# Sixteen expert weight slots refilled pair by pair, and 512-wide gate/up matmuls in a feed-forward

## The reference

```
def hier_moe(t, ...):            # 32 experts, hidden 512
    for e in range(N_EXPERTS):
        he = jax.nn.silu(t @ w_gate[e]) * (t @ w_up[e])
        y = y + combine[:, e:e + 1] * (he @ w_down[e])

def swiglu(x, w_in, w_out):      # 1024 -> 2 * 2816 -> 1024
    gate, up = jnp.split(x @ w_in, 2, axis=-1)
    return (jax.nn.silu(gate) * up) @ w_out
    # used as x = x + 0.5 * swiglu(rmsnorm(x, ...), ...), four times
```

## Time and profile before

| | |
|---|---|
| median of 3 runs | 1894.71 us (1894.43 to 1897.06) |
| profiled execution, its own time | 1897.47 us |
| its span, first to last instruction | 1895.6 us |
| TensorE (PE) busy | 1807.6 us (95%) |
| DVE busy | 938.3 us (49%) |
| ACT busy | 732.7 us (39%) |
| DMA | 441.92 MB, mean 233 GB/s |
| granted TensorE clock, mean | 0.983 |

### The profile page before, as it was taken

How to read it: one execution, slowest core, us unless ns; L and a number is a source line. 1 busy time by engine, 2 the same in 40 slices (tenths; PEclk the granted TensorE clock), 3 DMA queues, 4 the chain that set the end, 5 groups by cost and what they waited for, 6 DMA issues and landing times.

```text
span 1895.6 us, 29657 instructions
## 1 busy us (share of the span) xinstructions
PE 1807.6 (95%) x11498; PEld 1425.7 (75%) x11498; DVE 938.3 (49%) x1313; ACT 732.7 (39%) x1164; POOL 108.0 (6%) x121
## 2 busy tenths in 40 slices
PE   5999899999999879999999999999999998899998
PEld 2976544444434369998899998899989998779998
DVE  5773222222212265556877775545555554755554
ACT  2353212212212144444555554444444443754443
POOL 2010000000000000001212211000000001210000
PEclk8999899999999989999999999999999999999999
DMA  9966789999999966666554553556656665036663
GB/s 384 353 222 250 289 326 420 422 422 422 422 422 422 421 195 176 194 181 168 156 152 115 142 156 101 157 177 198 177 160 195 180 181 212 1 90 184 193 183 104
DMA packets 317570, 441.92 MB, mean 233 GB/s; under 512 B 12074, under 2 KB 270634, under 8 KB 289602
## 3 DMA queue, kind: packets, MB, share of 16 engines
q1 hardware_dynamic: 314418, 431.57, 66.0%
q0 software_dynamic: 2816, 8.45, 1.3%
q10 hardware_dynamic: 272, 1.05, 0.2%
HBM read 439.97 MB, written 1.05 MB: 233 GB/s over the span
## 4 chain that ended last, share of the span: by engine, by line
PE 79%; DMA 12%; DVE 4%; issue 2%; ACT 1%; POOL 1%; SPq 0%; POOLq 0%; DVEq 0%; ACTq 0%
PE PS L281 25%; PE PS L291 12%; PE PS L382 10%; DMA RAW<-w_up 9%; PE PS L2125 7%; PE PS L1712 4%; PE PS L2186 3%; PE PS L2099 2%; PE PS L158 2%; PE PS L1846 1%; PE PS L454 1%; DMA R<-w_down 1%; PE PS L528 1%; PE PS L511 1%; PE PS L719 1%
## 5 line engine op out<-in xcount | busy, mean ns | idle before, releaser
L281 PE MATMUL PS<-XH,LO 128*128 128x256 f32 x1344 | 380.3, 283 | 0.0
L281 PE MATMUL PS<-XL,HI 128*128 128x256 f32 x1344 | 380.3, 283 | 0.0
L281 PE MATMUL PS<-XH,HI 128*128 128x256 f32 x1344 | 379.9, 283 | 0.0
L203 DVE TENSOR_TENSOR LO<-RAW,HI 128x2048 fp32r<-128x2048 f32 x88 | 201.7, 2292 | 138.7 <-ACT HI L199 138.7
L281 PEld LDWEIGHTS PS<-XL,HI 128*128 128x128 f32 x1344 | 257.7, 192 | 3.1
L281 PEld LDWEIGHTS PS<-XH,HI 128*128 128x128 f32 x1344 | 257.7, 192 | 3.1
L281 PEld LDWEIGHTS PS<-XH,LO 128*128 128x128 f32 x1344 | 257.7, 192 | 0.0
L212 ACT ACTIVATE HI<-RAW 128x1024 fp32r<-128x1024 f32 x88 | 93.0, 1064 | 285.2 <-PE PS L291 285.2
L239 DVE TENSOR_TENSOR LO<-RAW,HI 128x1024 fp32r<-128x1024 f32 x88 | 107.5, 1225 | 186.5 <-ACT HI L212 186.5
L199 ACT ACTIVATE HI<-RAW 128x2048 fp32r<-128x2048 f32 x88 | 167.6, 1904 | 4.2 <-PE PS L1174 1.5
L291 PE MATMUL PS<-HI,HH 128*128 128x512 f32 x352 | 138.3, 393 | 0.4 <-DVE HL L247 0.2
(11 more groups left out here) (392 smaller groups left out, 3240.0 us busy)
## 6 DMA issues: line engine op xcount, KB each, us to landing
RAW<-ffn_w_in SPq DMA_DIRECT2D x176, 512.0 KB, 5.0
R<-w_gate SPq DMA_DIRECT2D x56, 1024.0 KB, 19.8
RAW<-ffn_w_out SPq DMA_DIRECT2D x88, 512.0 KB, 3.6
RAW<-a_w_in SPq DMA_DIRECT2D x69, 512.0 KB, 5.2
SPLIT<-w_up SPq DMA_DIRECT2D x31, 1024.0 KB, 21.9
RAW<-w_up SPq DMA_DIRECT2D x30, 1024.0 KB, 23.1
SPLIT<-w_down SPq DMA_DIRECT2D x30, 1024.0 KB, 17.9
R<-w_ada SPq DMA_DIRECT2D x24, 1024.0 KB, 10.7
```

The source lines that it names most:

```text
L203: v.tensor_tensor(M.LO[:, j, 0:2048], M.RAW[:, j, 0:2048], M.HI[:, j, 0:2048].bitcast(f32), ALU.subtract).then_inc(s.gu_lo[j], 1)
L281: m = e.matmul(GU[j][:, T * q:T * q + T], gu(w, j)[:, q, k, :], x[:, k, :], start=(k == 0 and n == 0), stop=(k == KT - 1 and n == 2))
```

## The change

**Experts.** The ring has sixteen slots in eight pairs: the six pairs of before, `MORE[0]` with `MORE[1]`, and `MORE[2]` with `MORE[3]`. They are refilled in the order `TURN`; pair p of loads waits for pair p - 8 to be used (`freed_by`), once for both loads. Since the place now differs from step to step, the 16 steps of SP's and of TensorE's program are written out where they were a loop. XH and XL are one tensor XHL, and their early users XH_SLOT and SPARE one XH_SPARE. The loads of norm_final and of the first feed-forward wait for 4, 0 and 2 loads of the last step.

```
+    TURN = (0, 1, 3, 4, 5, 6, 7, 2)
+    def freed_by(p):
+        return p - FIRST_PAIRS if p < FIRST_PAIRS + 2 else p - len(TURN)
...
+            for p in range(FIRST_PAIRS, PAIRS_IN):
+                sp.wait_ge(s.used, 2 * freed_by(p) + 2)
+                for x in range(2):
+                    first_load(2 * p + x)
...
-            with e.Fori(first // 2 or 1, end // 2 - 1) as i:
-                two_steps(i)
+                for i in range(end // 2 - 1):
+                    two_steps(i)
...
-            sp.wait_ge(M.steps.used, LOADS * (PAIR_STEPS - 1) + (8, 12)[j])
+            sp.wait_ge(M.steps.used, LOADS * (PAIR_STEPS - 1) + (0, 2)[j])
```

```
-                    for n, (w, x) in enumerate([(M.HI, XH), (M.HI, XL), (M.LO, XH)]):
-                        m = e.matmul(GU[j][:, T * q:T * q + T], gu(w, j)[:, q, k, :], x[:, k, :],
+                    e.matmul(GU[j][:, q].rearrange("p (w t) -> p w t", w=2), gu(M.HI, j)[:, q, k, :], XHL[:, k],
+                             start=k == 0, stop=False)
+                    m = e.matmul(HALF(j, 0)[:, q], gu(M.LO, j)[:, q, k, :], XH[:, k, :], start=False, stop=k == KT - 1)
...
+        def second_half(j, i):
+            a.activation(M.SECOND[:, j], HALF(j, 1), ACT.Copy).then_inc(s.silu[j], 1)
+        def step(j, i, following, after):          # ScalarE
+            second_half(j, i)
+            if following:
+                gu_high(*following)
+            silu(j, i)
+            if after:
+                dn_high(*after)
+            h_high(j, i)
...
+        def added(j, i):
+            v.tensor_tensor(M.GATE_UP[:, j], HALF(j, 0), M.SECOND[:, j], ALU.add).then_inc(s.h_done[j], 1)
+        def step(j, i, following, after):          # VectorE
+            added(j, i)
+            hidden(j, i)
+            if following:
+                gu_low(*following)
+            h_low(j, i)
+            if after:
+                dn_low(*after)
...
+        step(1, i - 1, (1, i), (0, i))             # ScalarE, i = 10
+        second_half(0, i)
         M.after(n_norm).first_high()
-        silu(1, FF_TWICE - 1)
+        silu(0, i)
+        dn_high(1, i)
+        h_high(0, i)
+        step(1, i, None, None)
```

More of the change, by code:

```diff
@@ L204, in gu_low, with dn_high @@
                         ALU.subtract).then_inc(s.gu_lo[j], 1)
-    def act():
[L207 to L212, removed]
-        def silu(j, i):
[L215 to L218, removed]
-            a.activation(M.HH[:, j], M.H[:, j], ACT.Copy).then_inc(s.hh_done[j], 1)
-        for j in range(2):
-            high_parts(j, 0, first=True)
+    def dn_high(j, i):
+        a.wait_ge(s.dn_in[j], i * 16 + (16 * u0 + 16))
+        a.wait_ge(s.dn_used[j], i + (u0 + 1))
+        a.activation(dn(M.HI, j), dn(M.RAW, j), ACT.Copy).then_inc(s.dn_hi[j], 1)
@@ L223, in act @@
         if f == 0:
             a.wait_ge(M.x_ready, 4)
[L225 to L230, removed]
+        first_silu()
+        gu_high(0, 1)
+        h_high(0, 0)
+        dn_high(1, 0)
+        with a.Fori(1, FF_TWICE - 1) as i:
+            step(1, i - 1, (1, i), (0, i))
+            step(0, i, (0, i + 1), (1, i))
+        i = FF_TWICE - 1
+        step(1, i - 1, (1, i), (0, i))
@@ L231, in act @@
+        second_half(0, i)
         M.after(n_norm).first_high()
-        silu(1, FF_TWICE - 1)
+        silu(0, i)
+        dn_high(1, i)
+        h_high(0, i)
+        step(1, i, None, None)
     def dve():
[L235 to L240, removed]
+        def added(j, i):
+            v.wait_ge(s.silu[j], i * 2 + (2 * u0 + 1))
+            v.tensor_tensor(M.GATE_UP[:, j], HALF(j, 0), M.SECOND[:, j], ALU.add).then_inc(s.h_done[j], 1)
@@ L251, in dve @@
             v.tensor_scalar(X[:, t], M.XNF[:, t], M.RSB[:, t:t + 1], None, ALU.mult).then_inc(M.x_ready, 2)
-        for j in range(2):
-            low_parts(j, 0, first=True)
+        dn_low(0, 0)
         hidden(0, 0, first=True)
[L255 to L259, removed]
+        h_low(0, 0)
+        gu_low(0, 1)
+        dn_low(1, 0)
+        with v.Fori(1, FF_TWICE - 1) as i:
+            step(1, i - 1, (1, i), (0, i))
+            step(0, i, (0, i + 1), (1, i))
+        i = FF_TWICE - 1
+        step(1, i - 1, (1, i), (0, i))
+        added(0, i)
+        hidden(0, i)
         M.after(n_norm).first_low()
-        hidden(1, FF_TWICE - 1)
+        h_low(0, i)
+        dn_low(1, i)
+        step(1, i, None, None)
         for n in range(4):
@@ L1917, in passes, with load @@
         extra = 1 if first else 0
-        def load(g, m, to=None, loaded=None):
+        def load(g, m, to, loaded):
             src = (gate, up, down)[m // 4][bass.ds(g * 2 + m % 2, 1), m // 2 % 2]
[L1921 to L1933, removed]
+            sp.dma_start(to, src.rearrange("e p n -> p (e n)")).then_inc(loaded, 16)
@@ L1935, in sync @@
         def sync():
             if first == 0:
[L1937 to L1960, removed]
+                first_pass_loads()
+                sp.wait_ge(s.used, LOADS * (PAIR_STEPS - 1) + 4)
+                sp.dma_start(M.NFR, A["norm_final"]).then_inc(M.mix.cx_in, 16)
+                return
@@ L2103, in w_loaded @@
         def w_loaded(i, odd, m):
[L2105 to L2111, removed]
+            if first == 0:
+                n = LOADS * (2 * i + odd) + m
+                at, loaded, count = home(n // 2, n % 2)
+                e.wait_ge(loaded, count)
+                return at
+            e.wait_ge(s.w_in[m // 2], i * (2 * 32) + 32 * (odd + 1 - PAIR_STEPS + pairs_on(m // 2)))
+            return SLOTS[m]
         def gate_up(i, odd):
@@ L2208, in pe @@
             if first == 0:
-                two_steps(0)
-            with e.Fori(first // 2 or 1, end // 2 - 1) as i:
-                two_steps(i)
+                for i in range(end // 2 - 1):
+                    two_steps(i)
+            else:
+                with e.Fori(first // 2, end // 2 - 1) as i:
+                    two_steps(i)
             it = end - 1
```

98 lines of the change are left out of this document (76 added, 22 removed).

## The result

The changed kernel takes 1886.01 us in the median of 5 runs (1883.86 to 1888.06). The kernel before took 1894.71 us in 5 runs beside it (1894.43 to 1899.48). The ratio is 0.9947 with a 95% interval of 0.9932 to 0.9961: 0.53% faster, some 10 us (the medians lie 8.7 apart), about half of the 20.2 that were forecast. The profiled executions took 1886.12 and 1897.47 us, 11.35 apart; what follows divides these.

A forecast was written before the change was run, and what follows sets the result against it. Experts were taken as bound by TensorE, then by DMA, the feed-forward by TensorE. Terms -8.35 - 14.0 + 2.1 = -20.2 us took 1894.71 to 1874.5 us; the 8-in-10 range was 1867 to 1889.

The forecast's parts named there:

- Thus none of the 8.35 us is left: Experts: sixteen slots let transfers start earlier, removing DMA's idle time between 245 and 275 us; -8.35 us.
- Edits at nothing: Experts: fetching TensorE's written-out steps as instructions costs nothing unless a fetch outlasts the work TensorE has queued; 0 us.
- A pair saves 2 x 119.8 - 229.2 = 10.4 ns: Feed-forward matmuls: one 512-wide replaces two 256-wide in each of 1344 pairs; -14.0 us in all.
- 1.9 us of cover are left: Feed-forward loop: other matmuls cover 8.3 us, so ACT's added copy and DVE's addition cost nothing in 80 steps.
- the chain of 6.4 us: Feed-forward step: ACT and DVE work between gate_up and its down product, summed with hops to 6.4 us.
- In the first step ... nothing: Feed-forward's first step: gu_high precedes h's high part, but the 3.5 us chain fits under gate_up's 5.6; costs nothing.
- The last down products: End of each feed-forward: copy and addition delay the last down product by 0.53 us, four times; +2.1 us.
- D: Rival, feed-forward loop: steps become bound by the chain through ACT and DVE; slower, 1916.5 us; chance 0.06.
- A: Rival, feed-forward: merged matmuls save nothing, as the long one's fixed part doubles with operand and target in two pieces; 1888.5 us; 0.12.
- C: Rival, feed-forward: the remaining 256-wide matmuls fall from 119.8 to 106.7 ns, 17.6 us more saved; 1856.9 us; chance 0.09.
- B: Rival, experts: earlier transfers bring nothing, as 14 loads ahead aren't possible or slots free too late; 1882.8 us; chance 0.09.
- the release by a w_down: Sign, end of experts: the last down product starts near 659.6 instead of 667.98, still waiting for a w_down load.

The follow-up runs named there:

- `e5_grouped`: Changed kernel with TensorE's expert steps 3 to 14 looped, plus each q's eight 512-wide matmuls before its eight 256-wide ones: 1876.96 us, ratio 0.9886.
- `e6_contiguous_x`: Changed kernel with TensorE's expert steps 3 to 14 looped, plus x's high and low halves side by side for each k: 1882.75 us, ratio 0.9922.
- the looped kernel: The changed kernel with TensorE's expert steps 3 to 14 in a loop of four steps, three turns, sixteen slots kept: 1882.06 us, ratio 0.9924.
- `e1_experts_only`: The changed kernel with the feed-forward of before, so only the experts' half of the change: 1891.46 us, ratio 0.9968 against the kernel before.

## Why the prediction was wrong

The direction and both mechanisms were right, and 1886.01 lies in the range, near its upper end. The size was off by a factor of two, and three steps of the working failed.

**"Thus none of the 8.35 us is left"** held: DMA ran full from 245 us, and the landings moved by 8.3 to 8.4 us. **"Edits at nothing: TensorE's steps written out must be fetched as instructions"** failed. The term was put at nothing, and the changed kernel loses 2.9 us of landings (3.06 - 0.12) with 10 fetches more. I asked only whether TensorE would wait for a fetch, and it doesn't. The fetch is itself a DMA transfer, and DMA had just been called the limit, at a share of 1.01. With nothing but the steps written out (12 fetches more) the kernel before lands its last load 1.8 us later (1.93 - 0.12); in the loop the last down product starts at 659.56, where the forecast had 659.4. That "the first steps of before were written out and ran at the same 28.20 us" was no evidence: there TensorE was the limit, not DMA.

**"A pair saves 2 x 119.8 - 229.2 = 10.4 ns"** was mis-sized: 6.8 measured. The rows were of matmuls among their own kind, x12 and x48; of alternating ones there was no row. With the rows' own conditions restored the pair saves 359.5 - 347.6 = 11.9 ns. The Trainium skill's rule of a fixed 2.5 ns ("TensorE: Matmul & The Clock Gate", section "Wait — 56ns, not 53.3ns?") agrees with neither: by it a pair would save 2.5, an estimate. Each matmul here has its own weights, and the fixed part was 10 ns and more (116.9 - 106.7).

**"1.9 us of cover are left, so the copy and the addition cost nothing in 80 steps"** failed in three of them, the ones that end in the second down product of the first, third and last feed-forward: 1.9 us. The cover itself was about right: a wait of ACT for the weights of 1.8 us opened no gap, waits of 2.12, 2.75 and 3.23 us opened 0.23, 0.58 and 1.06 us. But the chain of 6.4 us was summed from durations alone, and gu_high stands in it and waits for a load that had not landed. "In the first step ... nothing" held: the first down product had no gap.

**The last down products** were right, +0.53 forecast and +0.54 measured on average, by rows of each operation. That it agrees so closely is partly luck: one by one they were +0.61, +0.37, +0.43 and +0.74, since the forecast worked out the first feed-forward and took it four times. D's mechanism, the chain through ACT and DVE above its cover, showed itself in those three steps of 84 and not in the loop as a whole; A and C (0 or 23.5 ns per pair, against 6.8) fell. Of B the place was right: SyncE does get stuck in its issues, and no more than 12 loads were under way. But DMA stayed full with that, so it cost nothing. "DMA at 1.01 from about 241 us" and the gap at each last down product were seen; the release by a w_down, the step of 8.33 us and the 229 ns were not, and each of the three pointed at the failed step. Two of the signs of being wrong came too: a wait of TensorE for VectorE inside the loop, and a 256-wide matmul whose successor starts after 116.9 ns, not 120.

## What to carry over

Where DMA is the limit, count everything that goes through it, instruction fetches too: TensorE's steps written out added 10 to 12 here, and a loop over as many steps as the places need to repeat avoids them (41, against 40 before). A duration read from a row of equal instructions held among equals only; before you merge some of a kind, ask what will stand next to what, and group the widths. On ScalarE and VectorE put what TensorE waits for ahead of what waits for a load, even where the average step has cover: a chain is as long as its durations plus the wait for any load that stands in it.

## What the runs showed of the hardware

- Matmuls of 512 columns one after another, each with its own weights, start 228.7 ns apart, of 256 columns 118.9 ns (`e5_grouped`). In alternation it is 235.8 and 116.9, 5.1 ns more per pair. Why is open. Whether the operand is in one piece or two makes no difference (235.7 in `e6_contiguous_x`).
- 10 to 12 instruction fetches of 16 KB more, in a DMA at 421 GB/s, went with 1.8 to 2.9 us of later landings. Each is one packet that takes 1.0 to 1.1 us, so that 12 would be 0.8 us if their time were spread over the 16 DMA engines (an estimate).
- With 10 or 11 loads of 1 MB issued and not yet landed, SyncE's next issue takes 2.13 us in most cases (up to 6.05) instead of 0.33, and DMA stays full (422 GB/s from 550 to 600 us in the looped kernel). The most that were under way in any run are 13, in `e1_experts_only`.
